# Gate and up stage of a decoder layer: four seven-product units a block, a second set of sum buffers, two low parts by GpSimd

## What is computed

```python
D_FF = 5632
u = rmsnorm(h, pre_ffn_g[i])
ff = (jax.nn.silu(u @ w_gate[i]) * (u @ w_up[i])) @ w_down[i]
h = h + rmsnorm(ff, post_ffn_g[i])
```

## Time and profile before

| | before |
|---|---|
| median of three runs | 1076.29 us |
| the profiled execution | 1075.67 us |
| its span, first to last instruction | 1073.7 us |
| TensorE matmul busy | 1063.8 us (99%), 5731 instructions |
| VectorE busy | 891.5 us (83%) |
| ScalarE busy | 598.3 us (56%) |
| GpSimd busy | 31.5 us (3%) |
| mean granted TensorE clock | 0.999 |

### The profile page before, as it was taken

One profiled execution on the slowest core, in us unless ns is written; L12 is line 12 of the kernel. 1 busy time (PEld: TensorE's weight loads), 2 busy tenths in 40 slices (PEclk: granted clock), 3 DMA queues, 4 the chain that ended last, 5 costly groups with the idle time before them and its releaser, 6 DMA issues. The chain is left out here.

```text
span 1073.7 us, 15358 instructions
## 1 busy us (share of the span) xinstructions
PE 1063.8 (99%) x5731; PEld 921.6 (86%) x5731; DVE 891.5 (83%) x1082; ACT 598.3 (56%) x735; POOL 31.5 (3%) x49
## 2 busy tenths in 40 slices
PE   9999999999999999999999999999999999999997
PEld 8999999999888888888888888888888888888885
DVE  6699987646646787898998998988989899988887
ACT  6554454736545565555565655655655555655553
POOL 6000001101000000000000000000000000000000
PEclk9999999999999999999999999999999999999999
DMA  8655535444386475756756656657656666566665
GB/s 271 216 176 166 172 105 162 135 143 135 112 309 214 140 266 185 225 188 193 223 174 195 216 180 212 195 181 231 189 185 222 223 200 197 189 208 214 208 200 196
DMA packets 113208, 208.06 MB, mean 194 GB/s; under 512 B 9184, under 2 KB 46496, under 8 KB 111856
## 3 DMA queue, kind: packets, MB, share of 16 engines
q1 hardware_dynamic: 111952, 201.49, 58.8%
q10 hardware_dynamic: 608, 4.20, 1.0%
q0 software_dynamic: 576, 1.40, 0.4%
HBM read 202.86 MB, written 4.19 MB: 193 GB/s over the span
## 5 line engine op out<-in xcount | busy, mean ns | idle before, releaser
L561 ACT ACTIVATE w_hi<-raw 128x1024 fp32r<-128x1024 f32 x321 | 337.1, 1059 | 259.0 <-PE ps L1708 153.0
L910 DVE TENSOR_TENSOR w_lo<-raw,w_hi 128x1024 fp32r<-128x1024 f32 x321 | 389.6, 1226 | 84.0 <-ACT w_hi L561 83.4
L1706 PE MATMUL ps<-w_hi,uf 128*128 128x512 f32 x524 | 205.3, 392 | 0.1
L1708 PE MATMUL ps<-w_hi,uf 128*128 128x512 f32 x524 | 204.1, 389 | 0.0
L1707 PE MATMUL ps<-w_lo,uf 128*128 128x512 f32 x524 | 203.9, 389 | 0.0
L1377 PE MATMUL ps<-u,w_hi 128*128 128x272 f32 (+1 forms) x544 | 158.8, 292 | 0.0
L1379 PE MATMUL ps<-u,w_hi 128*128 128x272 f32 (+1 forms) x544 | 155.9, 287 | 0.0
L1380 PE MATMUL ps<-u,w_lo 128*128 128x272 f32 (+1 forms) x544 | 155.7, 286 | 0.0
L841 ACT CAST t_hi<-tx 128x1024 fp32r<-128x1024 f32 x92 | 96.4, 1053 | 67.7 <-DVE tx L1202 56.4
L1708 PEld LDWEIGHTS ps<-w_hi,uf 128*128 128x128 f32 x524 | 98.4, 188 | 20.6
L1706 PEld LDWEIGHTS ps<-w_hi,uf 128*128 128x128 f32 x524 | 98.4, 188 | 20.5 <-issue 0.5
(11 more groups left out here) (277 smaller groups left out, 1473.2 us busy)
## 6 DMA issues: line engine op xcount, KB each, us to landing
raw<-in_w_gate SPq DMA_DIRECT2D x176, 256.0 KB, 3.0
raw<-in_w_up SPq DMA_DIRECT2D x176, 256.0 KB, 3.5
raw<-in_w_down SPq DMA_DIRECT2D x88, 512.0 KB, 4.2
raw<-in_w_in SPq DMA_DIRECT2D x72, 512.0 KB, 3.6
raw<-in_w_out SPq DMA_DIRECT2D x32, 512.0 KB, 4.7
arena<-in_x SPq DMA_DIRECT2D x2, 1024.0 KB, 6.2
arena<-in_x ACTq DMA_DIRECT2D x2, 1024.0 KB, 8.7
out<-h2rows SPq DMA_DIRECT2D x2, 1024.0 KB, 5.5
```

What stands on the lines that cost most here:

```text
L561: act.activation(w_hi[:, slot, :], raw[:, slot, :], ACT.Copy).then_inc(hi_done, 1)
L910: dve.tensor_tensor(w_lo[:, slot, :], raw[:, slot, :], hi_view(w_hi[:, slot, :]), ALU.subtract).then_inc(lo_done, 1)
L1706: pe.matmul(o, a[0], b[0], start=start, stop=False)
L1708: return pe.matmul(o, a[1], b[0], start=False, stop=stop)
```

## The change

Blocks 1 to 7 have four Z, as units 1, 3, 5 and 6, and a fourth set of input sums is made in block 0. The weight sums get a second set of buffers (`tx2`, `t_hi2`, `t_lo2`), in the part of `ffn` that blocks 8 to 10 fill later; in blocks 1 to 7 the units take the second set and the first in turn, beginning with the second. `gated` moves there too. GpSimd makes the low part of two chunks a block in place of VectorE: of chunk 3 of blocks 1 to 7 (`IN_PRODUCT`, not before the first fold of the block) and of chunk 1 of blocks 2 to 8 (`IN_FOLD`, not before x0 is copied); `lo_pool` tells of them. At chunk 3 VectorE makes the weight sums first, then folds and inner products, then the low parts of the sums. `INNER_AT` is 4 in blocks 1 to 7. The core of the diff:

```diff
-    SEVEN_F, SEVEN_U = (0, 1, 2), (11, 12, 13, 14, 15, 16, 17, 18, 19)
+    SEVEN_F, SEVEN_U = (0, 1, 2, 3), (11, 12, 13, 14, 15, 16, 17, 18, 19)
-    F_SUM_AT = {10: 0, 12: 1, 14: 2}
-    ROUND = ["PPPPPPPP"] + ["PPZPZPZP"] * (NFG - 1) + [...]
+    F_SUM_AT = {10: 0, 12: 1, 13: 2, 14: 3}
+    WITH_SPARE = range(1, 8)
+    ROUND = ["PPPPPPPP"] + ["PZPZPZZP" if g in WITH_SPARE else "PPZPZPZP" for g in range(1, NFG)] + [...]
-    INNER_AT = 5
+    INNER_AT = [4 if g in WITH_SPARE else 5 for g in range(NFG + 1)]
+    IN_PRODUCT = {BEGIN[g] + 3: g for g in WITH_SPARE}
+    IN_FOLD = {BEGIN[g + 1] + 1: g for g in WITH_SPARE}
+    BY_POOL = sorted([*IN_PRODUCT, *IN_FOLD])
+    def buffers_of(z):
+        g, d = SEVENS[z]
+        return (z - SEVENS_TO[g - 1] + 1) % 2 if g in WITH_SPARE else 0
...
@@ SyncE
-                sp_eng.wait_ge(lo_done, q - WSLOTS + 1)
+                if q - WSLOTS in POOL_NO:
+                    sp_eng.wait_ge(lo_pool, POOL_NO[q - WSLOTS] + 1)
+                else:
+                    sp_eng.wait_ge(lo_done, lo_by_dve(q - WSLOTS))
@@ GpSimd
+            for q in BY_POOL:
+                slot = q % WSLOTS
+                if q in IN_FOLD:
+                    pool.wait_ge(x0_kept, IN_FOLD[q])
+                elif IN_PRODUCT[q] > 1:
+                    pool.wait_ge(fold_done, len(QUARTERS) * (IN_PRODUCT[q] - 2) + 1)
+                pool.wait_ge(hi_done, q + 1)
+                pool.tensor_tensor(w_lo[:, slot, :], raw[:, slot, :], w_hi[:, slot, :].bitcast(F32),
+                                   ALU.subtract).then_inc(lo_pool, 1)
@@ ScalarE
+                    elif q in IN_PRODUCT:
+                        weight_sums_hi(z)
+                        split(q)
@@ VectorE
+                    if q in IN_PRODUCT:
+                        weight_sums(q, z)
                     if 1 <= g <= NFG and ch == 3:
                         dve.wait_ge(chunks_used, BEGIN[g])
                         inner_product(g - 1)
-                    if z is None:
+                    if z is None and q not in POOL_NO:
                         split(q)
-                    elif ch % 2:
+                    elif q in IN_PRODUCT:
+                        weight_sums_lo(z)
+                    elif z is not None and ch % 2:
                         weight_sums(q, z)
                         split(q)
                         weight_sums_lo(z)
```

More of the change, by code:

```diff
@@ L153, in place_of, with lo_by_dve, before_in_buffers @@
         return g, ch, TURNS[g][ch // 2]
+    IN_PRODUCT = {BEGIN[g] + 3: g for g in WITH_SPARE}
+    IN_FOLD = {BEGIN[g + 1] + 1: g for g in WITH_SPARE}
+    BY_POOL = sorted([*IN_PRODUCT, *IN_FOLD])
+    POOL_NO = {q: i for i, q in enumerate(BY_POOL)}
+    def lo_by_dve(q):
+        return q + 1 - sum(1 for a in BY_POOL if a <= q)
+    def buffers_of(z):
+        g, d = SEVENS[z]
+        return (z - SEVENS_TO[g - 1] + 1) % 2 if g in WITH_SPARE else 0
+    def before_in_buffers(z):
+        return max((y for y in range(z) if buffers_of(y) == buffers_of(z)), default=None)
     def landed(q):
@@ L192, in build_trunk @@
         t_hi = sb_at("t_hi", [P, 4, DCOLS], F32R, a_xt + 16 * DCOLS)
+        a_spare = top[0] + 4 * KT * SEQ + 4 * 1152 + 4 * 4 * (max(WITH_SPARE) + 1) * 2 * SEQ
+        tx2 = sb_at("tx2", [P, 4, DCOLS], F32, a_spare)
+        t_lo2 = sb_at("t_lo2", [P, 4, DCOLS], F32R, a_spare)
+        t_hi2 = sb_at("t_hi2", [P, 4, DCOLS], F32R, a_spare + 16 * DCOLS)
+        sums_of, hi_of, lo_of = (tx, tx2), (t_hi, t_hi2), (t_lo, t_lo2)
         rows_u = tx[:, 0, :].rearrange("p (k t) -> p k t", k=2)
@@ L199, in build_trunk @@
         sums_f = sb_at("sums_f", [P, len(SEVEN_F), 4, 2, P], F32R, a_y)
-        gated = sb_at("gated", [P, NQ, DCOLS], F32, a_y + 4 * KT * SEQ - 8 * DCOLS)
+        gated = sb_at("gated", [P, NQ, DCOLS], F32, a_spare + 32 * DCOLS)
         sums_y = sb_at("sums_y", [P, max(len(SEVEN_U) - IN_U, 1), 3, 2, P], F32R, a_y)
-        assert 32 * P * len(SEVEN_F) + 8 * DCOLS <= 4 * KT * SEQ and 24 * P * (len(SEVEN_U) - IN_U) <= 4 * KT * SEQ
+        assert 32 * P * len(SEVEN_F) <= 4 * KT * SEQ and 24 * P * (len(SEVEN_U) - IN_U) <= 4 * KT * SEQ
         side = sb_at("side", [P, KT * SEQ], F32, a_y)
@@ L207, in build_trunk @@
         a_ff = place(4 * FT * 2 * SEQ)
+        assert a_spare == a_ff + 4 * 32 * 2 * SEQ and 32 * DCOLS + 8 * DCOLS <= 4 * 12 * 2 * SEQ
         ffn = sb_at("ffn", [P, FT, 2, SEQ], F32R, a_ff)
@@ L348, in build_trunk @@
             sem(n) for n in ("rows_done", "turned", "h2_hi", "h2_lo", "h2_sq", "r2c_done"))
+        lo_pool = sem("lo_pool")
         silu_done, p_done, f_hi, f_lo = (sem(n) for n in ("silu_done", "p_done", "f_hi", "f_lo"))
@@ L838, in weight_sums_hi @@
             def weight_sums_hi(z):
+                b = buffers_of(z)
                 for h in range(2):
                     act.wait_ge(t_made, 3 * z + h + 2)
-                    act.copy(t_hi[:, 2 * h:2 * h + 2, :], tx[:, 2 * h:2 * h + 2, :]).then_inc(t_hi_done, 1)
+                    act.copy(hi_of[b][:, 2 * h:2 * h + 2, :], sums_of[b][:, 2 * h:2 * h + 2, :]).then_inc(t_hi_done, 1)
             def row_sums_hi(d):
@@ L876, in _ @@
                         silu(g - 1)
-                    if 1 <= g <= NFG and ch == INNER_AT:
+                    if 1 <= g <= NFG and ch == INNER_AT[g]:
                         inner_hi(g - 1)
@@ L1212, in weight_sums_lo @@
                     dve.wait_ge(t_hi_done, 2 * z + h + 1)
-                    dve.tensor_tensor(t_lo[:, 2 * h:2 * h + 2, :], tx[:, 2 * h:2 * h + 2, :],
-                                      hi_view(t_hi[:, 2 * h:2 * h + 2, :]), ALU.subtract).then_inc(t_lo_done, 1)
+                    dve.tensor_tensor(lo_of[b][:, 2 * h:2 * h + 2, :], sums_of[b][:, 2 * h:2 * h + 2, :],
+                                      hi_view(hi_of[b][:, 2 * h:2 * h + 2, :]), ALU.subtract).then_inc(t_lo_done, 1)
             def four_sums(i, hi, lo, r, s):
@@ L1716, in right, with weights_split @@
                 return [w_hi[:, q % WSLOTS, at], w_lo[:, q % WSLOTS, at]]
+            def weights_split(q):
+                if q in POOL_NO:
+                    pe.wait_ge(lo_pool, POOL_NO[q] + 1)
+                else:
+                    pe.wait_ge(lo_done, lo_by_dve(q))
             def plain_products(q, quarters):
@@ L1720, in plain_products @@
                 kt, chs = 2 * d + ch % 2, 2 * len(ROUND[g])
-                pe.wait_ge(lo_done, q + 1)
+                weights_split(q)
                 if g >= NFG:
@@ L1740, in weight_sum @@
                 def weight_sum(t):
-                    return [t_hi[:, t, :], t_lo[:, t, :]]
-                pe.wait_ge(lo_done, q + 1)
+                    return [hi_of[buffers_of(z)][:, t, :], lo_of[buffers_of(z)][:, t, :]]
+                weights_split(q)
                 if g < NFG:
```

29 lines of the change are left out of this document (16 added, 13 removed).

## The result

The changed kernel takes 1084.24 us (median of 6 runs, 1083.33 to 1085.47), the one before 1075.8 us beside it. The ratio is 1.0078, with a 95% interval of 1.0068 to 1.0089: 8.4 us slower, where 7.1 were forecast. The profiled execution took 1085.32 us, its span is 1083.6.

A forecast was written before the change was run, and what follows sets the result against it. TensorE, busy for 99% of the span, was taken as the bound. A net 5.7 us in blocks 2 to 7 plus 1.4 in block 1 gave +7.1 on 1075.67: 1082.8 us, range 1077.0 to 1088.0.

The forecast's parts named there:

- Removed: On TensorE, one product of three matmuls fewer in each of seven blocks: 0.68 us a block, 4.76 us in all.
- The deciding wait: TensorE stalls 1.63 us for VectorE's inner low part: net +0.95 us a block in blocks 2 to 7, 5.7 us.
- m6: A block's first product into a bank of the transposes on TensorE; due at S+9.03, forecast to start at S+10.67.
- f_lo: VectorE's low part of the transposed inner tiles, which empties the bank m6 needs; forecast at S+10.48.
- The port: VectorE operations on two SBUF tiles wait for GpSimd's part: low parts 0.46 us later; GpSimd's part taken as 2.3 us.
- Block 1: No folds, but a ScalarE table load; inner products start at S+4.96, stall 2.08 us, net +1.4 us.
- S: Start of a block on TensorE, 5.45 us before its transposes; the prediction's times count from it.
- The loads: Loads still released by the low parts in the old order; claimed to cost nothing.
- (a): Rival: same wait without the port, VectorE and GpSimd overlapping freely; +4.3 us, 1080.0; chance 0.27.
- (b): Rival: chain up to f_lo shorter than its rows say, so the change gains, at most 4.76 us; chance 0.10.
- (d): Rival: stalls of about the 0.68 us won, so within 2.15 us of before; chance 0.08.
- (c): Rival: VectorE becomes the bound, period 44.4 us, +2.0 for seven blocks, 1089.9; chance of such large losses 0.06.

The follow-up runs named there:

- third_x0: third_unit with ScalarE copying x0 ahead of its split of chunk 1 in blocks 2 to 8: 1072.07 us, ratio 0.9964.
- inner_first: The change with VectorE making the inner tiles' low part ahead of the split of chunk 4 in blocks 1 to 7: 1081.96 us, ratio 1.0055.
- product_by_dve: The change with chunk 3's low part back on VectorE in blocks 1 to 7: 1092.01 us, ratio 1.0155.
- third_unit: The change with the first Z (seven-product unit) of blocks 1 to 7 as the third unit, inner tiles at chunk 5: 1073.96 us, ratio 0.9976.
- split_first: The change with ScalarE splitting chunk 3 ahead of the two weight-sum copies in blocks 1 to 7: 1080.7 us, ratio 1.0046.
- inner_x0: inner_first with ScalarE copying x0 ahead of its split of chunk 1 in blocks 2 to 8: 1080.19 us, ratio 1.0045.
- third_unit_3z: third_unit with three Z a block and three sets of input sums, as before the change: 1075.78 us, ratio 0.9998.
- third_no_pool: third_x0 with all low parts made by VectorE, none by GpSimd: 1087.26 us, ratio 1.0116.

## Why the prediction was right, and where not

**Removed.** 21 matmuls and 0.68 us a block: right. third_x0, with the same seven-product units and no such wait, has blocks of 41.7 to 42.0 us from block 3 on.

**The deciding wait.** Right in place, cause and size. TensorE idles at m6 once in each of blocks 1 to 7, until the inner low part. The net in an ordinary block is 43.23 - 42.37 = 0.86 us, forecast 0.95; the chain up to f_lo was 0.07 shorter than summed, and the release cost 0.16 (0.05 to the start of m6, and the next matmul 0.34 behind it in place of 0.227) in place of 0.2. The idle time itself reads 1.14 to 1.18, just under the 1.2 to 1.9 given as a sign: the stall of 1.54 (the net and the 0.68 won) also holds the tail that the profile counts for the matmul ahead, the slower start behind, and 0.1 from late transposes. Taking one split out of that chain (inner_first) left 0.3 us of the wait, adding one (product_by_dve) made the block longer by 0.68, and moving the unit (third_unit) made the kernel faster than before.

**The port.** Right: 0.48 us measured, 0.46 said. It had rested on one colliding pair; split_first (no overlap, 2.35) and product_by_dve (no GpSimd, 2.35) against 2.83 confirm it from two sides. In inner_x0 a sum lost 0.49 to it, and in block 1 of split_first GpSimd came second and lost 0.3. The rule of the Trainium skill (SBUF — State Buffer, "Who interferes with whom"), by which the second to come waits for the first, agrees in all of them, also for the operations with one SBUF input. The loss is not quite the whole overlap: in block 3 VectorE lost 0.48 where the profile has the two together for 0.62. GpSimd's part took 2.38 to 2.42 us in all 14 places, 2.3 said.

**Block 1.** Mis-sized: net +1.4 said, 2.4 measured, 1.9 ahead of its transposes and 0.5 behind them. The step that failed is "now the split is behind t_hi, at S+1.81", which has the weight sums start at S-2.4. VectorE's first sum started at S-1.4, when chunk 3's load had landed, at 411.59 (the profile names no releaser):

```profile
408.81 2.36 DVE L952 TENSOR_TENSOR w_lo<-raw,w_hi 128x1024 fp32r<-128x1024 f32 x2
411.67 0.69 DVE L1241 TENSOR_TENSOR tx<-raw 128x512 f32<-128x512 f32 x1 [0.51 <-issue]
...
418.96 1.41 DVE L1213 SCALAR_TENSOR_TENSOR gated<-ps,cst,gated 128x512 f32<-128x512 f32 x2 [4.13 <-ACT gated L856]
```

Here S is 413.03, without the wait for the inner product. All behind the sum is 0.8 to 1.0 later than summed. In the trace of before that load landed at 410.72, S-1.3, and nothing needed it then. The load is half of it: VectorE itself came to the sum only at 411.17, S-1.9, behind two splits (408.81) that stand behind the low part of the fourth set of input sums. The prediction had put that set at nothing.

**The loads.** Also wrong was the "Nothing" behind the sentence that the loads are still released "in the old order". The order is the old one, the time is not. VectorE has the sums of two seven-product units in a row to make ahead of the low part that releases the load of the next block's chunk 1. In blocks 2 to 8 of the kernel before that load lands 7.6 to 8.5 us before S, after the change 6.7 to 7.2 before it in the ordinary blocks; it is issued some 1.2 us later. That the fourth unit does it is shown by third_unit_3z and third_unit, which differ in that unit and its input sums: chunk 1's load is issued 13.2 us before S in the one and 9.3 in the ordinary blocks of the other. The split of chunk 1 takes 1.06 us and has to be done by S-5.2, so 0.5 to 1 us is left. In blocks 2 and 4 the load took 6.0 and 5.8 us in place of 4.1 to 4.5 and used that up. A load of 4.8 us in block 4 of the kernel before cost nothing. So the late release took the margin, which every block shows; why those two loads were slow is open. That x0 behind that split carries the delay on is shown by third_x0. The same holds for the load of chunk 3, which the weight sums now need at S-1.85: it landed at S-2.1 to S-2.8 in blocks 2 to 7, just in time, and in inner_first and inner_x0 it was late.

The two waits cost the profiled execution 1.3 us in blocks 2 and 4. They are one reason why the blocks took 8.9 us and not 7.1: 1.3 is of these, 1.0 of block 1, and 0.09 less in each of the six others takes 0.5 off.

**The sum.** Of the 9.9 us between the two spans, the blocks account for 8.9: 1.9 up to the transposes of block 1, 7.0 in the seven distances behind them. The other 1.0 is there before any changed instruction: the same matmul of the first stage (L1480, now L1529) starts at 18.27 in the one profile and at 19.25 in the other. It differs from one execution to the next: the first matmul of the gate and up stage starts between 363.5 and 365.3 in the profiles of the ten kernels with the change's code ahead of it. The median, 1.1 below that execution, is the better measure: 8.4.

**The rivals.** (a) no port wait: fell, by the length of the pair. (b) faster: fell with the f_lo chain. (d) nothing comes of it: fell, 8.4 us are clear of the 2.15. (c) VectorE the bound: not in this arrangement, where VectorE is busy for 40.66 of 43.23 us and waits 1.47 us for x0; it is what third_no_pool runs into.

## What to carry to other kernels

When a step is moved forward on the busiest engine, list the buffers it writes and ask for each when the last reader is done, in the order of that reader's own engine, and list the loads it reads and ask for each when it lands; here a bank freed by the thirteenth VectorE instruction behind the fold sums cost more than the matmuls saved. Keep an operation that a long chain waits for (x0) ahead of one that waits for a load in the same queue. Here GpSimd took work from VectorE for nothing beside operations that read PSUM, and for most of the overlap (0.48 of 0.62 us) beside those that read two SBUF tiles.

## What was not expected of the hardware

In blocks 1 to 7 a few loads of 256 KB take 5.3 to 6.5 us from issue to landing where most take 2.5 to 4.9. They occur before the change too (two issued at 660.3 and 661.4, 5.7 and 5.8 us) and cost nothing there; the profiles of split_first, inner_x0 and third_unit_3z have none. In two profiles they stand 86 to 87 us apart (528.7 and 614.7 in third_unit, 446.5 and 533.8 after the change), which is also two blocks: all four are the load of a chunk 1. Why they are slow was not looked into.
